# A transformer block pair on one core: norms and modulation go piece by piece into the operand's split, the feed-forward norm's reciprocal multiplies the first product's result, and first panels go tile by tile

## Chip, cores and metric

The kernel runs on one core of one Trainium2 chip. The metric is the device time of one execution in microseconds; the median of three runs is given. The profile is one execution of the same program.

## What is computed

One input of 256 tokens by 1024 features goes through two blocks. The first has an RMS norm, a state-space branch, an attention branch, gates and a feed-forward part. The second has two layers, each with a modulation of its input, three branches and a layer norm. What the change touches:

```
h = h + merged @ w_out                                   # first block
hid = relu(rmsnorm(h, norm_mlp) @ w_ff1)
h = h + (hid * hid) @ w_ff2
h = rmsnorm(h, norm_final)
for l in 0, 1:                                           # second block
    u = h * (1 + scale) + shift                          # shift, scale, gate: c_act @ w_ada + b_ada
    proj = u @ w_in                                      # q_lat, kv_lat, k_rope, ... are columns of proj
    ...
    h = layer_norm(ALPHA * h + gate * (m @ w_o), ln_g, ln_b)
```

`rmsnorm(x, g) = x * rsqrt(mean(x * x) + eps) * g`.

## The kernel before, in words

Activations stand transposed: features over the 128 partitions in 8 tiles (KT), 256 tokens in the free dimension. `h` is the residual stream. Every product is exact to about fp32 by three fp32r matmuls per tile (`three`, L1573 to L1575): both weights and operand are split in a high half (a rounding copy to fp32r) and a low half (value minus high half).

Weights come in panels, mostly 1024 rows by 256 columns (1 MB). The program `schedule` writes the order of everything by hand into one list; each engine walks through that list and executes its own part of each step. So the order of the list is the order in each engine's queue. A panel has five stages: SP loads it into one of four raw slots (L651); scalar makes the high half `w_hi` (L803); vector (L1082), or for `gate`, `ff1` and `ff2` GpSimd (L711), makes the low half `w_lo`; TensorE waits for that low half and does 48 matmuls of 256 columns in two column blocks (`blocks`); scalar or vector empties the bank. The halves of a panel are made ahead, by `next_splits`: at the step of a weight panel up to the panel three further in `w_hi`'s three slots and under four further in the index of all panels, at the step of an `ada` panel under two further in the index. The `ada` panels (the modulation's weights) count in the index, though they are not split; TensorE multiplies them as they land.

The operand is split too. `u_hi`, `u_lo` (L782, L1091) are shared by all panels of a stage and made in four pieces of two tiles. `low` makes one piece of the low half once scalar has its high half. The first panel of a stage waits for the four pieces at its tiles 0, 2, 4, 6 of the first column block.

Stages around the change:

- Start: `norm(0)`: scalar squares, TensorE sums with a matrix of ones (L1663), scalar takes the root (L782, with a table load), vector the reciprocal (L1127), then eight multiplies (L1140) into `tmp`, four high and four low pieces.
- Feed-forward (`ff1`, `ff2`): `out` panels add to `h` (L1109); `norm_steps(1, "u2", 14)` sets three `ada` panels between the last sum and the first `ff1` panel, while the norm goes on. Then eight chunks of two `ff1` and two `ff2` panels. Vector takes relu of a bank (L1356), scalar squares it and makes its high half, vector the low half.
- Into layer 0 of the second block: `norm_steps(2, ("u", 0), 17)`: the last norm of the first block writes into `h`, then `modulate(0)` on vector (L1418) makes `tmp`, whose rows vector subtracts the high half from, while scalar makes the same rows from `h` straight into `u_hi`.
- Into layer 1: `ln(0)` multiplies `h` by `rstd` (L1545); `modulate(1)` as above, with the layer norm's gain and bias folded into scale and shift by `modulate_columns(1)`.
- `prescale` (layer 0) or `ln_affine` (layer 1) multiply `h` by ALPHA on scalar, beside the latent sums.

The low half of the panel after `ada` panels (`ff1` 0, `q_lat` 0) is made in the step of the last of these three. In the list this is after `norm` or `ln`, and before `modulate`.

## Time and profile before

| | |
|---|---|
| median of three runs | 1257.37 us (1255.42 to 1257.55) |
| the profiled execution | 1257.67 us, span 1255.9 us |
| TensorE matmul busy | 1097.3 us, 87% |
| vector busy | 762.3 us, 61% |
| scalar busy | 536.6 us, 43% |
| GpSimd busy | 253.0 us, 20% |
| mean granted TensorE clock | 0.909 |

The span is the time from the first to the last instruction; the run's time has 1.8 us around it. TensorE is the busiest engine, but its busy time holds matmuls at two clock levels. Where it idles, the profile names what it waited for; where the granted clock is below 1, its matmuls start further apart.

### The profile page before, as it was taken

To read this page: it belongs to the slowest core of one execution; us is meant where nothing else is said; L and a number is where in the kernel's file an instruction comes from. 1 tells how busy PE (TensorE), PEld (TensorE's weight loads), DVE (VectorE), ACT (ScalarE), POOL (GpSimd) and SP (SyncE) were. 2 spreads that over 40 slices of the span, in tenths; PEclk is the share of its full clock that TensorE was granted. 3 is DMA by queue.
4 is the path that set the end of the run, shared out by engine and by line. 5 is a ranking of instruction groups with operands and counts; after the bars stand their busy time and mean duration, and the time that the engine had idled before them with its cause. 6 is when DMAs were issued, how large, how long until landed. Compare 5 with 4: busy or idle time off the path is not lost.

```text
span 1255.9 us, 19600 instructions
## 1 busy us (share of the span) xinstructions
PE 1097.3 (87%) x8120; PEld 1012.5 (81%) x8120; DVE 762.3 (61%) x1111; ACT 536.6 (43%) x613; POOL 253.0 (20%) x125
## 2 busy tenths in 40 slices
PE   5989779788989999979968798999799688989995
PEld 4976557667889999969867698998688687889985
DVE  4947556655353523255687788665556977795652
ACT  4533334253244444345423363643465132635432
POOL 2094753000078878700000000000000000000000
PEclk7977797788989999989979899999899788999998
DMA  7532332165566565545523345464447142545610
GB/s 250 186 102 90 112 125 77 68 201 180 167 195 197 168 200 169 182 128 190 172 68 101 101 143 161 136 213 153 131 139 235 38 131 76 160 137 166 202 35 33
DMA packets 159431, 179.53 MB, mean 143 GB/s; under 512 B 4976, under 2 KB 141680, under 8 KB 159344
## 3 DMA queue, kind: packets, MB, share of 16 engines
q1 hardware_dynamic: 159024, 177.22, 44.6%
q8 instruction: 64, 1.05, 0.4%
q0 software_dynamic: 320, 1.07, 0.2%
q14 instruction: 23, 0.19, 0.0%
HBM read 177.23 MB, written 1.05 MB: 142 GB/s over the span
## 4 chain that ended last, share of the span: by engine, by line
PE 58%; DVE 23%; issue 7%; ACT 7%; POOL 3%; DMA 1%; DVEq 0%; SPq 0%; ACTq 0%; POOLq 0%
PE pg L1573 17%; PE pg L1574 16%; PE pg L1575 16%; DVE area L1473 7%; DVE area L1091 5%; ACT w_hi L803 3%; DVE w_lo L1082 3%; ACT area L782 2%; DVE area L1099 2%; PE p_y L1729 1%; PE p_s L1663 1%; DVE mx L1494 1%; PE p_s L1712 1%; DVE area L1109 1%; DMA raw<-in_w_in 1%
## 5 line engine op out<-in xcount | busy, mean ns | idle before, releaser
L1573 PE MATMUL pg<-u_hi,w_hi 128*128 128x256 f32 x1664 | 497.7, 299 | 40.3 <-DVE u_lo L1091 36.0
L1574 PE MATMUL pg<-u_lo,w_hi 128*128 128x256 f32 x1664 | 487.3, 293 | 0.0
L1575 PE MATMUL pg<-u_hi,w_lo 128*128 128x256 f32 x1664 | 486.3, 292 | 0.0
L1573 PEld LDWEIGHTS pg<-u_hi,w_hi 128*128 128x128 f32 x1664 | 336.5, 202 | 53.0 <-issue 44.7
L1574 PEld LDWEIGHTS pg<-u_lo,w_hi 128*128 128x128 f32 x1664 | 336.8, 202 | 0.8
L1575 PEld LDWEIGHTS pg<-u_hi,w_lo 128*128 128x128 f32 x1664 | 335.9, 202 | 0.0
L1082 DVE TENSOR_TENSOR w_lo<-raw,w_hi 128x2048 fp32r<-128x2048 f32 (+3 forms) x109 | 241.2, 2218 | 115.0 <-ACT w_hi L803 114.8
L803 ACT ACTIVATE w_hi<-raw 128x2048 fp32r<-128x2048 f32 (+2 forms) x147 | 272.5, 1857 | 79.7 <-issue 38.6
L711 POOL TENSOR_TENSOR w_lo<-raw,w_hi 128x2048 fp32r<-128x2048 f32 x38 | 175.9, 4646 | 220.5 <-ACT w_hi L803 220.5
L809 ACT ACTIVATE area<-pg 128x512 f32<-128x512 f32 (+2 forms) x92 | 54.0, 587 | 168.9 <-PE pg L1575 156.9
L1473 DVE SCALAR_TENSOR_TENSOR area<-area,par 128x256 f32<-128x256 f32 x240 | 97.8, 479 | 0.8
L1573 PE MATMUL pg<-vb_hi,w_hi 128*128 128x256 f32 (+1 forms) x320 | 90.8, 284 | 1.4 <-POOL w_lo L711 0.9
L1575 PE MATMUL pg<-vb_hi,w_lo 128*128 128x256 f32 (+1 forms) x320 | 90.5, 283 | 0.0
L1574 PE MATMUL pg<-vb_lo,w_hi 128*128 128x256 f32 (+1 forms) x320 | 90.4, 282 | 0.0
L1573 PE MATMUL pg<-va_hi,w_hi 128*128 128x256 f32 x288 | 84.1, 292 | 1.8 <-DVE w_lo L1082 0.8
L1574 PE MATMUL pg<-va_lo,w_hi 128*128 128x256 f32 x288 | 83.3, 289 | 0.0
L1575 PE MATMUL pg<-va_hi,w_lo 128*128 128x256 f32 x288 | 83.1, 289 | 0.0
L1091 DVE TENSOR_TENSOR area<-area 128x512 f32<-128x512 f32 (+7 forms) x86 | 55.0, 639 | 30.7 <-ACT area L809 27.3
L782 ACT ACTIVATE area<-area 128x384 f32<-128x384 f32 (+6 forms) x67 | 37.1, 553 | 79.3 <-DVE area L1356 50.1
L1109 DVE TENSOR_TENSOR h<-pg,h 128x512 f32<-128x512 f32 x36 | 24.9, 691 | 66.5 <-PE pg L1575 65.6
L782 ACT ACTIVATE area<-area,nmax 128x128 f32<-128x128 f32 (+1 forms) x32 | 14.5, 455 | 112.7 <-DVE nmax L1095 112.2
L1573 PEld LDWEIGHTS pg<-vb_hi,w_hi 128*128 128x128 f32 (+1 forms) x320 | 60.0, 187 | 2.1 <-POOL w_lo L711 1.1
(211 smaller groups left out, 1338.3 us busy)
## 6 DMA issues: line engine op xcount, KB each, us to landing
raw<-in_w_in SPq DMA_DIRECT2D x68, 1024.0 KB, 5.5
raw<-in_w_ff SPq DMA_DIRECT2D x32, 1024.0 KB, 5.6
raw<-in_w_ada SPq DMA_DIRECT2D x24, 1024.0 KB, 5.2
raw<-in_w_gate SPq DMA_DIRECT2D x8, 1024.0 KB, 7.7
raw<-in_w_o SPq DMA_DIRECT2D x8, 1024.0 KB, 5.2
raw<-in_w_out SPq DMA_DIRECT2D x4, 1024.0 KB, 6.6
raw<-in_w_b_out SPq DMA_DIRECT2D x4, 1024.0 KB, 5.1
raw<-in_w_c_out SPq DMA_DIRECT2D x4, 1024.0 KB, 5.6
```

The costliest lines, as they stand in the source:

```text
L711: pool.tensor_tensor(w_lo[:, s, 0:n], raw[:, r, 0:n], w_hi[:, s, 0:n].bitcast(F32), ALU.subtract).then_inc(sem(f"raw_free{r}"), 1)
L782: return act.activation(out_, in_, func, **kw)
L803: act.activation(w_hi[:, q["s"] % HL, 0:n], raw[:, q["index"] % RAW, 0:n], ACT.Copy).then_inc(*c.event("w_hi", q["s"]))
L809: act.activation(dst, src, func, **kw).then_inc(*c.bank_free(g))
L1082: dve.tensor_tensor(w_lo[:, s, 0:n], raw[:, r, 0:n], w_hi[:, s, 0:n].bitcast(F32), ALU.subtract).then_inc(sem(f"raw_free{r}"), 1)
L1091: return dve.tensor_tensor(out_, a, b, op)
L1099: return dve.scalar_tensor_tensor(out=out_, in0=a, scalar=s, in1=b, op0=op0, op1=op1)
L1109: dve.tensor_tensor(out_, a, b, op).then_inc(*c.bank_free(g))
L1473: ins = dve.scalar_tensor_tensor(out=acc[:, j, :], in0=apad[:, j, k:k + T], scalar=w, in1=acc[:, j, :], op0=ALU.mult, op1=ALU.add)
L1573: pe.matmul(dst, w_h, x_h, start=first, stop=False)
L1574: pe.matmul(dst, w_h, x_l, start=False, stop=False)
L1575: return pe.matmul(dst, w_l, x_h, start=False, stop=last_)
```

## The change

1. `blocks`: where a panel waits for more than one piece, the order is by tile first and column block second, so that 12 matmuls instead of 6 can follow each piece. The start flag is set only by the very first.
2. The feed-forward norm. `u2_piece(j)`: scalar writes h times the gain into `u_hi`, vector the low half straight from h. No reciprocal is in it; it is multiplied to the relu of `ff1`'s result. The sums, root and reciprocal come after the pieces. The `ada` panels 15 and 16 move behind `ff1` 0 and 1.
3. `scaled`: vector multiplies `h` by `rstd` in four pieces, and makes the low halves between. The last norm of the first block no longer has its gain in `h`; it goes into the modulation's columns and into `prescale`, as in layer 1.
4. `modulate` moves from vector to scalar: two Identity into `tmp` and one Copy into `u_hi` a piece.

```diff
@@ def norm_steps
         ada_panel(i + 2)
         step("ada_turn", i + 1)
-        if k == 2:
-            step("modulate", 0)
-        step("split", key)
+        step("modulate", key[1])
         step("ada_take", i + 2)
@@ schedule, before and in the feed-forward
-    norm_steps(1, "u2", 14)
+    step("u2_piece", 0)
+    ada_panel(14)
+    norm_sums(1, 3)
+    for j in range(1, 4):
+        step("u2_piece", j)
+    step("ada_take", 14)
+    step("norm", 1)
     chunks = DFF // W
     for c in range(chunks + 1):
         if c < chunks:
             for n in range(2):
                 panel("ff1", 0, 2 * c + n, "w_ff1", 0, W * c + 256 * n, KT, 256, 1)
-                if (c, n) == (0, 0):
+                if c == 0:
+                    step("ada_turn", 14 + n)
+                    ada_panel(15 + n)
+                    step("ada_take", 15 + n)
+                if (c, n) == (1, 0):
                     step("ada_turn", 16)
                     step("ada_end", 1)
@@ scalar
+            def u2_piece(j, _):
+                if j == 0:
+                    act.wait_ge(sem("groups"), OPERANDS["u2"]["after"] + 1)
+                for s, v in emptied([groups_of("out")[j]]):
+                    act.wait_ge(s, v)
+                for i in (2 * j, 2 * j + 1):
+                    fn(u_hi[:, i, :], h[:, i, :], ACT.Identity, scale=col("norm_mlp", i)).then_inc(*(c.event("hi", "u2", j) if i % 2 else c.step()))
+
+            def modulate(l, _):
+                o = OPERANDS["u", l]
+                act.wait_ge(sem("groups"), o["after"] + 1)
+                act.wait_ge(sem("scale1"), over("scale1", l))
+                for j in range(4):
+                    act.wait_ge(sem("ln_rows"), over("ln_rows", l - 1, j))
+                    for i in (2 * j, 2 * j + 1):
+                        fn(tmp[:, i, :], h[:, i, :], ACT.Identity, bias=shift1[:, i:i + 1],
+                           scale=scale1[:, i:i + 1]).then_inc(*c.step())
+                    fn(u_hi[:, 2 * j:2 * j + 2, :], tmp[:, 2 * j:2 * j + 2, :], ACT.Copy).then_inc(*c.event("hi", ("u", l), j))
@@ scalar, prescale
-                act.wait_ge(sem("rows"), over("rows", ("u", l), 3))
-                fn(h[:, :, :], h[:, :, :], ACT.Copy, scale=ALPHA).then_inc(*c.event("alpha_h", l))
+                for j in range(KT):
+                    fn(h[:, j, :], h[:, j, :], ACT.Identity, scale=rest_g[:, j:j + 1]).then_inc(*(c.event("alpha_h", l) if j == KT - 1 else c.step()))
@@ vector: norm(k) calls scaled(-1) for k == 2, ln(l) calls scaled(l)
+            def scaled(l):
+                before = c.last
+                for j in range(4):
+                    dve.wait_ge(*before)
+                    dve.tensor_tensor(h[:, 2 * j:2 * j + 2, :], h[:, 2 * j:2 * j + 2, :], spread(rstd[:, 0, :], P, 2, T),
+                                      ALU.mult).then_inc(*c.event("ln_rows", l, j))
+                    if j and l < LAYERS - 1:
+                        low(("u", l + 1), j - 1)
+                if l < LAYERS - 1:
+                    low(("u", l + 1), 3)
+
+            def u2_piece(j, _):
+                dve.wait_ge(sem("hi"), over("hi", "u2", j))
+                for i in (2 * j, 2 * j + 1):
+                    stt(u_lo[:, i, :], h[:, i, :], col("norm_mlp", i), u_hi[:, i, :].bitcast(F32), ALU.mult,
+                        ALU.subtract).then_inc(*(c.event("lo", "u2", j) if i % 2 else c.step()))
@@ vector, panel, job ff1
-                    dve.tensor_scalar(tmp[:, f:f + 2, :], both, 0.0, None, ALU.max).then_inc(*c.bank_free(g))
+                    dve.scalar_tensor_tensor(out=tmp[:, f:f + 2, :], in0=both, scalar=0.0, in1=spread(rstd[:, 0, :], P, 2, T),
+                                             op0=ALU.max, op1=ALU.mult).then_inc(*c.bank_free(g))
@@ TensorE, blocks
-                for i, (a, m) in enumerate(widths):
-                    for k in range(q["kt"]):
-                        if i == 0 and k in waits:
-                            pe.wait_ge(*waits[k])
-                        ins = three(pg[g % 2][0:m, i * T:i * T + T], wh[:, k, a:a + m], wl[:, k, a:a + m],
-                                    x_hi[:, k, :], x_lo[:, k, :], k == 0, k == q["kt"] - 1)
+                turns = [(i, k) for i in range(len(widths)) for k in range(q["kt"])]
+                mixed = len(waits) > 1
+                if mixed:
+                    turns.sort(key=lambda at: at[1])
+                for i, k in turns:
+                    a, m = widths[i]
+                    if i == 0 and k in waits:
+                        pe.wait_ge(*waits[k])
+                    ins = three(pg[g % 2][0:m, i * T:i * T + T], wh[:, k, a:a + m], wl[:, k, a:a + m],
+                                x_hi[:, k, :], x_lo[:, k, :], k == 0 and not (mixed and i),
+                                (i, k) == turns[-1] if mixed else k == q["kt"] - 1)
```

`modulate_columns(0)` now also runs, in the third chunk of the feed-forward: it puts the last norm's gain into `scale1` and `rest_g`, and `shift1` is copied.

## Rows read from the trace of the kernel before

**Rows 1.** Busy engines (the page), and TensorE's waits (total, times, longest us).
```profile
PE 1097.3 (87%) x8120; PEld 1012.5 (81%) x8120; DVE 762.3 (61%) x1111; ACT 536.6 (43%) x613; POOL 253.0 (20%) x125
PE pg L1573 <- DVE u_lo L1091: 36.0, 6, 9.1
```
**Rows 2.** Timelines around F: start us, us, what, idle before, releaser.
```profile
337.20 0.69 DVE L1109 TENSOR_TENSOR h<-pg,h 128x512 f32<-128x512 f32 x1 [5.92 <-PE pg L1575]
337.93 0.63 ACT L782 ACTIVATE area<-h 128x512 f32<-128x512 f32 x1 [5.98 <-DVE h L1109]
339.62 1.28 ACT L782 ACT_TABLE_LOAD   x1
341.94 1.90 ACT L803 ACTIVATE w_hi<-raw 128x2048 fp32r<-128x2048 f32 x1
343.92 4.49 POOL L711 TENSOR_TENSOR w_lo<-raw,w_hi 128x2048 fp32r<-128x2048 f32 x1 [124.08 <-ACT w_hi L803]
350.03 0.55 PE L1573 MATMUL pg<-u_hi,w_hi 128*128 128x256 f32 x1 [6.87 <-DVE u_lo L1091]
359.96 0.39 PE L1573 MATMUL pg<-u_hi,w_hi 128*128 128x256 f32 x1 [0.59 <-POOL w_lo L711]
```
**Rows 3.** Clock by stretch: PE, PEld, DVE, ACT, POOL busy, clock, DMA share, GB/s.
```profile
350.10:356.10 6.00, 6.00 (x26) 5.60 (x27) 3.44 (x7) 4.32 (x5) 0.80 (x1) 0.50 0.53 192
556.50:561.00 4.50, 4.50 (x20) 4.39 (x21) 3.14 (x7) 4.01 (x8) 0.00 (x0) 0.50 0.46 160
```
**Rows 4.** Timeline of TensorE at M, the first `w_o` panel of layer 0.
```profile
860.53 0.35 PE L1573 MATMUL pg<-u_hi,w_hi 128*128 128x256 f32 x1 [3.08 <-DVE u_lo L1091]
...
861.20 0.28 PE L1575 MATMUL pg<-u_hi,w_lo 128*128 128x256 f32 x1
861.31 0.41 PE L1573 MATMUL pg<-u_hi,w_hi 128*128 128x256 f32 x1
861.52 0.41 PE L1574 MATMUL pg<-u_lo,w_hi 128*128 128x256 f32 x1
```
**Rows 5.** Vector: L1140 and L1109 (min/median/max ns), and the relu of 360 to 545.
```profile
L1140 DVE SCALAR_TENSOR_TENSOR area<-h,par,rows x16: 471/478/4775, 19.6 to 351.8; 128x256 f32<-128x256 f32 x16
L1109 DVE TENSOR_TENSOR h<-pg,h x31: 690/691/693, 381.0 to 537.8; 128x512 f32<-128x512 f32 x31
L1356 DVE TENSOR_SCALAR area<-pg 128x512 f32<-128x512 f32 x15 | 10.4, 691 | 45.1 <-PE pg L1575 44.9
```
**Rows 6.** Timelines around Q0, and the landing time of `w_in` loads (the page).
```profile
546.53 1.75 DVE L1127 RECIPROCAL rows<-root 128x256 f32<-128x256 f32 x1 [5.17 <-ACT root L782]
547.13 1.90 ACT L803 ACTIVATE w_hi<-raw 128x2048 fp32r<-128x2048 f32 x1
551.49 2.28 DVE L1082 TENSOR_TENSOR w_lo<-raw,w_hi 128x2048 fp32r<-128x2048 f32 x1
556.41 0.55 PE L1573 MATMUL pg<-u_hi,w_hi 128*128 128x256 f32 x1 [8.06 <-DVE u_lo L1091]
raw<-in_w_in SPq DMA_DIRECT2D x68, 1024.0 KB, 5.5
```
**Rows 7.** Timelines around Q1.
```profile
899.41 5.45 ACT L782 ACTIVATE u_hi<-h,shift,scale 128x256 fp32r<-128x256 f32 x8
900.44 2.28 DVE L1082 TENSOR_TENSOR w_lo<-raw,w_hi 128x2048 fp32r<-128x2048 f32 x1
904.96 0.55 PE L1573 MATMUL pg<-u_hi,w_hi 128*128 128x256 f32 x1 [5.81 <-DVE u_lo L1091]
```
**Rows 8.** Timelines: `prescale`, `ln_affine`, and TensorE behind the latter.
```profile
578.50 1.91 ACT L782 ACTIVATE h<-h 128x2048 f32<-128x2048 f32 x1
926.86 5.46 ACT L782 ACTIVATE h<-h,rest_b,rest_g 128x256 f32<-128x256 f32 x8
941.31 0.39 PE L1573 MATMUL pg<-u_hi,w_hi 128*128 128x256 f32 x1 [0.56 <-DVE w_lo L1082]
```
**Rows 9.** Timeline of TensorE's weight loads at S: a wait for the second piece.
```profile
23.73 0.29 PEld L1573 LDWEIGHTS pg<-u_hi,w_hi 128*128 128x128 f32 x1 [0.17 <-DVE u_lo L1091]
```

More of the change, by code:

```diff
@@ L236, in schedule @@
             step("rope_tables")
+            step("modulate_columns", 0)
     for j in range(3):
@@ L335, in schedule @@
             step("modulate", 1)
-            step("split", ("u", 1))
             step("ada_take", 23)
@@ L823, in split @@
                     act.wait_ge(sem("groups"), o["after"] + 1)
-                if isinstance(key, tuple) and key[0] == "u":
-                    l = key[1]
-                    act.wait_ge(sem("scale1"), over("scale1", l))
-                    for j in range(KT):
-                        if l == 0:
-                            act.wait_ge(sem("h_rows"), over("h_rows", j))
-                        else:
-                            act.wait_ge(sem("ln_rows"), over("ln_rows", l - 1, j // 2))
-                        fn(u_hi[:, j, :], h[:, j, :], ACT.Identity, bias=shift1[:, j:j + 1],
-                           scale=scale1[:, j:j + 1]).then_inc(*(c.event("hi", key, j // 2) if j % 2 else c.step()))
-                    return
                 if key == "ctx":
@@ L1046, in ln_affine @@
                     if l < LAYERS - 1:
-                        act.wait_ge(sem("rows"), over("rows", ("u", l + 1), j // 2))
                         fn(h[:, j, :], h[:, j, :], ACT.Identity, bias=rest_b[:, j:j + 1],
@@ L1054, in ln_affine @@
                            bias=col(("ln_b", l), j), scale=col(("ln_g", l), j)).then_inc(*c.event("affine", l, j))
-            steps = dict(split_ahead=split_ahead, silu=silu, norm_squares=norm_squares, norm=norm, ada_take=ada_take, ln_centre=ln_centre,
+            steps = dict(split_ahead=split_ahead, silu=silu, norm_squares=norm_squares, norm=norm, ada_take=ada_take, ln_centre=ln_centre, u2_piece=u2_piece, modulate=modulate,
                          ln_affine=ln_affine, split=split, panel=panel, gate_ahead=gate_ahead, s5_sines=s5_sines, s5_turn=s5_turn, s5_y=s5_y, s5_inner=s5_inner,
@@ L1130, in norm @@
                 invert(("norm", k))
-                name = ("norm_mix", "norm_mlp", "norm_final")[k]
                 if k == 0:
                     dve.wait_ge(sem("par_landed"), 16)
-                key = ("u0", "u2", None)[k]
+                    before = c.last
+                    for j in range(KT):
+                        dve.wait_ge(*before)
+                        ins = dve.scalar_tensor_tensor(out=tmp[:, j, :], in0=h[:, j, :], scalar=col("norm_mix", j), in1=rstd[:, 0, :],
+                                                       op0=ALU.mult, op1=ALU.mult)
+                        ins.then_inc(*(c.event("rows", "u0", j // 2) if j % 2 else c.step()))
+                        if j % 2 and j >= 3:
+                            low("u0", j // 2 - 1)
+                    low("u0", 3)
+                elif k == 2:
+                    scaled(-1)
+            def scaled(l):
                 before = c.last
-                for j in range(KT):
+                for j in range(4):
                     dve.wait_ge(*before)
-                    dst = tmp[:, j, :] if k < 2 else h[:, j, :]
-                    ins = dve.scalar_tensor_tensor(out=dst, in0=h[:, j, :], scalar=col(name, j), in1=rstd[:, 0, :],
-                                                   op0=ALU.mult, op1=ALU.mult)
-                    ins.then_inc(*(c.event("h_rows", j) if k == 2 else c.event("rows", key, j // 2) if j % 2 else c.step()))
-                    if k < 2 and j % 2 and j >= 3:
-                        low(key, j // 2 - 1)
-                if k < 2:
-                    low(key, 3)
+                    dve.tensor_tensor(h[:, 2 * j:2 * j + 2, :], h[:, 2 * j:2 * j + 2, :], spread(rstd[:, 0, :], P, 2, T),
[9 more added lines that the diff above has]
+                        ALU.subtract).then_inc(*(c.event("lo", "u2", j) if i % 2 else c.step()))
             S = lambda k: small[:, k, :]
@@ L1541, in ln @@
                 invert(("var", l))
-                before = c.last
-                for j in range(4):
-                    dve.wait_ge(*before)
-                    dve.tensor_tensor(h[:, 2 * j:2 * j + 2, :], h[:, 2 * j:2 * j + 2, :], spread(rstd[:, 0, :], P, 2, T),
-                                      ALU.mult).then_inc(*c.event("ln_rows", l, j))
+                scaled(l)
             dve.wait_ge(sem("const"), over("const", "all"))
```

28 lines of the change are left out of this document (10 added, 18 removed).

## Prediction

> **What bounds the kernel now.** I first read the engine shares: TensorE is busy 1097.3 us of 1255.9, vector 762.3 [rows 1]. TensorE sets the pace, so an edit is worth what it does to TensorE's idle time and clock. Then the waits of TensorE: its largest entry is 36.0 us in six waits of a weight panel for `u_lo`, the low half of the shared operand [rows 1]. The change touches exactly the six places of these waits. I call them by what follows: S (first panel), F (feed-forward), Q0 and Q1 (first panel of layers 0 and 1 of the second block), M (`w_o`, twice). TensorE idles 6.87 us before F, 8.06 before Q0, 5.81 before Q1, 3.08 before M [rows 2, 4, 6, 7]. Third, the granted clock after them: it is 0.50 from 350.1 to 356.1 and from 556.5 to 561.0 [rows 3], the level of 1.2 GHz; after Q1's idle time it lasts to about 909. Neighbouring matmuls start 0.21 us apart at the low level, 0.12 at the high one [rows 4]. A panel of 48 takes 5.8 us at the high level, and each microsecond spent at the low level costs 0.44 us (4.7 matmuls, worth 0.56). Last, the timelines of vector, scalar and GpSimd at the five kinds of place give the order of things.
>
> **F before.** Sum, table load, root, reciprocal, rows. TensorE starts `ff1` 0 at 350.03 and ends it near 358.9; `ff1` 1 starts at 359.96, when GpSimd has its low half [rows 2], so `ff1` 2 ends two panels later, near 371.6.
>
> **F after.** `u2_piece` needs no norm. The last `out` group ends near 337.1, its rows are in h at 337.89 [rows 2]. Scalar: an Identity of one tile takes 0.68 in a row of eight (5.46) [rows 8], so piece 0 stands at 338.45, the square (0.63) [rows 2] at 339.1, pieces 1 to 3 at 340.5, 341.9, 343.2. Vector adds two steps of 0.48 [rows 5] and a handover: low halves at 339.5, 341.5, 342.9, 344.3. The weights of `ff1` 0 are early: it is now three places behind `out` 2 instead of six, so its high half is made in that step and GpSimd is through near 331. TensorE ends the sums at 340.2 and takes 12 matmuls (1.44) a piece, at the high level: 341.7, 343.15, 344.6, 346.05. That is 12.8 us earlier than 358.9, by the norm's chain taken off the path and the new order of tiles.
>
> Most of it is lost again at once. `ff1` 1 is four places behind `out` 3 and the look-ahead takes less than four. So its high half is made in the step of `ff1` 0, and scalar comes to that after the pieces (343.2), `ada_take` 14 (0.4), the table load (1.28) [rows 2] and the root (0.4): 345.4. High half 1.90, to 347.3; GpSimd 4.49, a little more in steady state, to 352.0 [rows 2]. TensorE has `ada` 15 behind it at 347.4: a new idle time of 4.6 us. I expect the clock to fall: the idle times of 5.81 to 8.06 did that, and even 3.08 before M was followed by starts 0.21 apart [rows 4]. Taking 4.7 us at the low level, as after Q0, costs 2.1. So `ff1` 1 ends at 359.9, `ada_turn` and `ada` 16 at 361.3, `ff1` 2 at 367.0, one more turn makes 367.4 against 371.6. **Gain 4.2 us.** Bounds: 6.3 if the clock stays high, 3 if it is low for 6.1 us as after F before, and GpSimd late by half a microsecond.
>
> The relu now multiplies by `rstd` too. No row shows this form. Below: the relu itself, 0.691, and the addition of a bank and an SBUF tile, 0.691 as well. Above: two half-width scalar_tensor_tensor, 0.96 [rows 5]. I take 0.7, the nearest row being the addition with its two operands of the same kinds. It is hidden: vector idled 45.1 us before 15 relus [rows 5]; without that cover the upper bound would make 16 x 0.27 = 4.3 us. GpSimd, busy in most of this stretch, might hold it: a multiply on two SBUF operands at F lasted 4.775 (median 0.478). But the 31 additions from 381 to 538, with a bank and an SBUF tile, never took over 0.693 [rows 5]. I take no hold.
> The Trainium skill (SBUF — State Buffer, "SBUF: two separate sides") states a lock between vector and GpSimd, and for a vector instruction not in a fast mode names two SBUF inputs as its condition. By that rule the new multiply, with one input in PSUM, runs free and the sum stays; a rule without this condition would speak against the change and give case (c) below. The trace agrees with the page: 4.775 for two SBUF inputs, 0.693 at most for one.
>
> **Q0 and Q1.** Before, vector did the norm's rows, then `w_lo` of the first panel (2.28, at 551.49 and 900.44), then modulation and low halves [rows 6, 7]. Now `scaled` does the rows and all four `low` calls, inside `norm` or `ln`. The first panel's `w_lo` belongs to the step of an `ada` panel further down, so in vector's queue it stands behind all four pieces. And pieces are slower: scalar makes them alone, two Identity and a Copy (0.68 + 0.68 + 0.72 with its gap), 2.1 us each, 8.4 for four. Before, scalar's share was 5.45 [rows 7].
> Q0: scalar is free at 549.05, the first rows stand at 549.0 (reciprocal to 548.3, one step of 0.7) [rows 6]. Pieces end at 551.2, 553.3, 555.4, 557.4; last low half 558.15; `w_lo` to 560.4. TensorE starts at 560.5 instead of 556.41, 4.1 later, and no longer waits between pieces (about 0.4 before). **Loss 3.7 us.** Bounds 2.8 and 5: the time at the low level may be 1 us shorter or 2 longer, and the pieces a little off.
> Q1: scalar starts at 899.41 as before [rows 7]. Last piece 907.8, low half 908.5, `w_lo` 910.75, TensorE at 910.85 instead of 904.96: 5.9, less 0.2 of waits inside. **Loss 5.7 us**, bounds 4.5 and 6.9.
> Behind the waiting `low` calls vector has only this `w_lo` and later ones queued, and TensorE alone waits for them. Scalar's queue has `ada_take` and the next high halves behind the pieces; they are done (about 561 in Q0) well before TensorE, now at 568, wants them. On SP's queue the load into the raw slot that is freed 7 to 10 us later belongs to the fourth panel after, over 15 us on; it lands in 5.5 [rows 6]. Free. The tile order gives nothing here, since every piece is there at the start.
>
> **The rest.** `prescale` is 8 steps, 5.46, instead of one of 1.91. Layer 1 does that already, and there TensorE idles 0.56 at 941.31; layer 0 has no such gap [rows 8]. Loss 0.6, bounds 0 and 1.2. `modulate_columns(0)`, five small steps, lies in F, where vector idles: nothing. S: each wait for a piece costs 0.1 to 0.2 at the low level [rows 9], some 0.5 in three; the new order takes them away. Gain 0.3, bounds 0 and 0.6. M: no piece is waited for after the first, TensorE being slower (six matmuls 1.28) than the pieces come (0.8): nothing, bounds 0 and 0.2. `out` 0 has all pieces in advance. The last `scaled(1)` is the old code.
>
> **Sum**, against this execution (1257.67: span 1255.9 and 1.8 around it; the median of three is 1257.37, 0.3 less): -0.3 - 4.2 + 3.7 + 5.7 + 0.6 = +5.5, so **1263.2**. All good ends together give +0.2 (-0.8 - 6.3 + 2.8 + 4.5 + 0, 1257.9), all bad ones +10.1 (1267.8).
>
> **The rivals.**
> (a) Faster. The first panel's `w_lo` isn't behind the pieces but between or before them, and TensorE takes 12 matmuls as each piece comes. Then Q0 starts at 552.0 and ends at 560.3, not 564.4 (-4.1), and Q1 ends at 910.0, not 912.8 (-2.8); sum -0.3 - 4.2 - 4.1 - 2.8 + 0.6 = -10.8, 1246.9. For it: before, `w_lo` came right behind the rows [rows 6, 7], and scalar's half was made by 549.03. Against it: the `low` calls now stand ahead of it in one queue. The point from which it decides is the start of `w_lo` before the last `u_lo`. Chance 0.10.
> (b) No change. The stall before `ff1` 1 doesn't come, because its high half is made before table load and root; F gains 4.6 + 2.1 more, 1256.5. Against it: in the old trace too the high half came after the table load (339.62, 341.94) [rows 2]. Chance 0.12.
> (c) Still slower. The relu's multiply is held by GpSimd as the norm's was. A hold is 4.3 at most; with half of it hidden by the other bank for a quarter of the sixteen, 8 to 9 more, 1272. Against it: the additions [rows 5]. Chance 0.06.
> The forecast keeps 0.72.
>
> **From this to the numbers.** The likeliest case gives 1263.2. The range of 8 in 10 goes from 1256.5, which takes in (b) and my lower bound, to 1268.5, above my upper bound; (a) and (c) stay out. A measurement of this kernel tells about 0.2% (2.5 us) from no change: faster is under 1254.9, slower over 1259.9. Faster: (a) and a little of (b), 0.12. Same: the rest of (b) and my low end, 0.16. Slower: 0.72.
>
> **What the new profile would show.** F: `ff1` 0 starts near 340 with no idle time of note, then one of 4 to 5 us released by GpSimd's `w_lo`. Q0 and Q1: TensorE idles about 12 us and is released by vector's `w_lo`, no longer by `u_lo`. The relu's rows stay near 0.7. If TensorE's wait at Q0 still ends with `u_lo`, or `ff1` 1 follows without a gap, the prediction is wrong.

## The result and the profile after

The changed kernel takes 1262.67 us (median of 20 runs, 1255.54 to 1270.18). The kernel before takes 1257.48 in the 20 runs beside it. The ratio is 1.0043, with a 95% interval of 1.0025 to 1.0061: slower by 5.2 us, where 5.5 was forecast. The profiled execution of the changed kernel took 1261.53; its span is 1259.8, against 1255.9.

First the engine shares of the changed kernel and, from the view of TensorE's waits, the entries of weight panels (total us, times, longest).

```profile
PE 1098.5 (87%) x8120; PEld 1012.3 (80%) x8120; DVE 746.9 (59%) x1089; ACT 545.8 (43%) x632; POOL 252.9 (20%) x125
```
```profile
PE pg L1594 <- DVE w_lo L1097: 24.0, 5, 11.7
PE pg L1594 <- DVE u_lo L1106: 15.8, 3, 9.7
```

Before, one entry of 36.0 us named `u_lo` [rows 1]. Now 24.0 us name vector's `w_lo`, the low half of a weight panel, and `u_lo` keeps 15.8 in three waits. TensorE's busy time grew by 1.2 us (0.1%), the span by 3.9: most of the difference is idle time, and it has a new releaser.

F. Timelines of the changed kernel for scalar, vector, GpSimd and TensorE (start us, us, what, idle before and its releaser), in this order.

```profile
335.04 1.05 ACT L790 ACTIVATE u_hi<-h,par 128x256 fp32r<-128x256 f32 x2 [5.25 <-PE pg L1596]
336.18 0.63 ACT L790 ACTIVATE area<-h 128x512 f32<-128x512 f32 x1
336.91 3.34 ACT L790 ACTIVATE u_hi<-h,par 128x256 fp32r<-128x256 f32 x6
340.36 0.39 ACT L817 ACTIVATE root<-pg 128x256 f32<-128x256 f32 x1
340.84 1.28 ACT L790 ACT_TABLE_LOAD   x1
342.14 0.38 ACT L790 ACTIVATE root<-p_s 128x256 f32<-128x256 f32 x1
342.42 1.90 ACT L811 ACTIVATE w_hi<-raw 128x2048 fp32r<-128x2048 f32 x1
```
```profile
335.04 0.69 DVE L1124 TENSOR_TENSOR h<-pg,h 128x512 f32<-128x512 f32 x1 [5.92 <-PE pg L1596]
344.42 0.69 DVE L1389 SCALAR_TENSOR_TENSOR area<-pg,rows 128x512 f32<-128x512 f32 x1
```
```profile
344.40 9.52 POOL L719 TENSOR_TENSOR w_lo<-raw,w_hi 128x2048 fp32r<-128x2048 f32 x2 [15.91 <-ACT w_hi L811]
```
```profile
348.97 0.38 PE L1594 MATMUL pg<-u_hi,w_hi 128*128 128x256 f32 x1 [3.89 <-POOL w_lo L719]
```

The idle 6.87 us ahead of `ff1` 0 [rows 2] are gone: `ff1` 0 runs from 337.65 to 343.74 without a pause. Behind it and the short `ada` 15 TensorE stands still from 345.08 on for 3.89 us. The rows say why, read backwards: it waits for GpSimd's low half, which began at 344.40; that waited for the high half of 342.42 on scalar, and ahead of it in scalar's queue stand the pieces, `ada_take` 14 (scalar empties that panel's bank), the table load and the root, one right after the other from 336.91 on.

The two first panels of the second block, TensorE's timeline:

```profile
552.53 0.58 PE L1594 MATMUL pg<-u_hi,w_hi 128*128 128x256 f32 x1 [11.73 <-DVE w_lo L1097]
...
907.97 0.58 PE L1594 MATMUL pg<-u_hi,w_hi 128*128 128x256 f32 x1 [11.10 <-DVE w_lo L1097]
```

and vector's timeline ahead of Q0:

```profile
540.76 1.29 DVE L1167 TENSOR_TENSOR h<-h,rows 128x512 f32<-128x512 f32 x2
543.62 0.69 DVE L1106 TENSOR_TENSOR u_lo<-area,u_hi 128x512 fp32r<-128x512 f32 x1 [1.57 <-ACT u_hi L790]
...
549.58 0.69 DVE L1106 TENSOR_TENSOR u_lo<-area,u_hi 128x512 fp32r<-128x512 f32 x1 [1.29 <-ACT u_hi L790]
550.19 5.62 DVE L1097 TENSOR_TENSOR w_lo<-raw,w_hi 128x2048 fp32r<-128x2048 f32 x3
```

The idle time was 8.06 and 5.81 us and ended with `u_lo` [rows 6, 7]. Now it is 11.73 and 11.10 and ends with `w_lo`. Vector was through with the rows' first half at 542.05 and then waited for scalar before each of four low halves, 4.2 us in all, with `w_lo` behind them in its queue though its input had been ready since 541.57. This is what the forecast named.

Where the 3.9 us of span come from, by landmarks that both traces have (the last sum of `out` into `h`, the start of TensorE's idle time at Q0 and at Q1, and the first matmul of the sums of the latents, the norm that follows `q_lat`):

| landmark | before | after | difference so far | the stretch itself |
|---|---|---|---|---|
| last sum of `out` | 337.20 | 335.04 | -2.2 | -2.2 |
| idle time at Q0 begins | 548.35 | 540.80 | -7.6 | F: -5.4 |
| sums of the latents, layer 0 | 578.46 | 574.85 | -3.6 | Q0: +3.9 |
| idle time at Q1 begins | 899.15 | 896.87 | -2.3 | +1.3 |
| sums of the latents, layer 1 | 926.82 | 930.08 | +3.3 | Q1: +5.5 |
| end of span | 1255.9 | 1259.8 | +3.9 | +0.6 |

The first line isn't the change's. The experiment `block2_part_only`, whose code up to there is the old one, has the same landmark at 334.99, and `tiles_only`, which has the new start, has it at 337.20. The granted clocks from 12 to 30 us differ (0.54 before, 0.72 in the changed kernel, 0.72 and 0.54 in these two). The +1.3 between the latents and Q1 isn't a term of the change either. It holds a stretch of low clock, 575.1 to 578.5, which the kernel before doesn't have there: the ten matmuls of the sums take 4.11 us instead of 2.43. Six of the fourteen traces have such a stretch at these sums, `ff_part_only` among them, whose `prescale` is the old one, so it doesn't come with the eight steps. Rows of the changed kernel by stretch (busy us of PE, PEld, DVE, ACT and POOL, then granted clock, DMA share, GB/s):

```profile
350.00:353.50 3.50, 3.50 (x19) 3.50 (x19) 0.00 (x0) 1.91 (x1) 3.50 (x1) 0.54 0.94 306
353.50:357.00 3.50, 3.50 (x36) 3.40 (x39) 0.49 (x1) 0.00 (x0) 3.50 (x2) 1.00 0.01 4
552.50:558.30 5.80, 5.77 (x28) 5.78 (x29) 3.31 (x2) 0.29 (x1) 0.00 (x0) 0.52 0.80 245
575.30:578.70 3.40, 3.40 (x11) 2.69 (x9) 0.00 (x0) 3.17 (x8) 0.00 (x0) 0.53 0.63 173
908.00:913.20 5.20, 5.20 (x25) 5.20 (x26) 3.25 (x2) 0.23 (x1) 0.00 (x0) 0.52 0.82 248
```

After the new idle time at F TensorE restarted at 348.97; the clock was at its low level (1.2 GHz) from 349.8 for about 3.4 us, and then at the high one (2.4 GHz): 19 matmuls in 3.5 us, then 36.

### The profile page after: what moved, and what is told of

Its sections match the earlier page's. It is cut to its first block, busy times and chain, and to the rows that moved or that the text cites. A ratio compares the mean times of both kernels' runs of the same rounds, so it can differ in the third digit from the quotient of the medians.

```text
span 1259.8 us, 19580 instructions
## 1 busy us (share of the span) xinstructions
PE 1098.5 (87%) x8120; PEld 1012.3 (80%) x8120; DVE 746.9 (59%) x1089; ACT 545.8 (43%) x632; POOL 252.9 (20%) x125
## 4 chain that ended last, share of the span: by engine, by line
PE 58%; DVE 23%; ACT 8%; issue 7%; POOL 3%; DMA 1%; DVEq 0%; SPq 0%; ACTq 0%; POOLq 0%
PE pg L1594 16%; PE pg L1595 16%; PE pg L1596 16%; DVE area L1498 7%; DVE area L1106 5%; ACT w_hi L811 4%; DVE w_lo L1097 3%; ACT area L790 2%; DVE area L1114 2%; PE p_s L1690 2%; PE p_y L1756 1%; PE p_s L1588 1%; DVE mx L1519 1%; PE p_s L1739 1%; DVE area L1124 1%
## 5 line engine op out<-in xcount | busy, mean ns | idle before, releaser
L1106 DVE TENSOR_TENSOR area<-area 128x512 f32<-128x512 f32 (+7 forms) x86 | 55.0, 639 | 30.2 <-ACT area L817 26.5
```

Source lines behind the costliest of these rows:

```text
L1106: return dve.tensor_tensor(out_, a, b, op)
```

## The experiments

### The two halves of the change, each alone

`ff_part_only` is the kernel before with everything at F: `u2_piece`, the new order of steps, the relu that multiplies by `rstd`, and the tile order of first panels. `block2_part_only` has only the second block's part: the modulation of both layers on scalar, the columns of layer 0 made earlier, `scaled` with its `low` calls, and the eight steps of `prescale`.

```diff
 ff_part_only, against before
-    norm_steps(1, "u2", 14)
+    step("u2_piece", 0)
+    ada_panel(14)
+    norm_sums(1, 3)
+    for j in range(1, 4):
+        step("u2_piece", j)
+    step("ada_take", 14)
+    step("norm", 1)
...
 block2_part_only, against before
+        if k == 2:
+            step("modulate", 0)
+        else:
+            step("split", key)
...
-                fn(h[:, :, :], h[:, :, :], ACT.Copy, scale=ALPHA)
+                for j in range(KT):
+                    fn(h[:, j, :], h[:, j, :], ACT.Identity, scale=rest_g[:, j:j + 1])
```

> The kernel before with the feed-forward part of the change (pieces of the operand without the norm, reciprocal in the relu, ada panels 15 and 16 moved) and the tile order, nothing of the second block. My theory: TensorE idles about 4 us before ff1 1 instead of 6.9 before ff1 0, the place gives 4.2 to 5.5 us, the tile order about 1 more (waits between pieces at the start and before both q_lat panels gone): 1251 to 1252.5. Rival, that the multiply on rstd is held by GpSimd: relu rows of over 1 us and no gain, 1257 or more.

> The changed kernel with the feed-forward part and the tile order put back: only scaled, the modulation on scalar, the columns and prescale in eight steps. My theory: TensorE idles about 12 us before each first q_lat panel (8.1 and 5.8 before), released by vector's w_lo; 3.7 + 5.7 + 0.6 to 1.7, so 1267 to 1269. Rival, that the loss of the whole change comes from somewhere else (clock phases, the feed-forward part): 1257 to 1260.

Measured: `ff_part_only` 1254.04 (1251.59 to 1255.78, ratio 0.9965, interval 0.9953 to 0.9978), `block2_part_only` 1273.89 (1268.03 to 1274.44, ratio 1.0108, interval 1.0089 to 1.0126). TensorE's timeline in both:

```profile
348.10 0.39 PE L1603 MATMUL pg<-u_hi,w_hi 128*128 128x256 f32 x1 [3.88 <-POOL w_lo L721]
547.99 0.55 PE L1603 MATMUL pg<-u_hi,w_hi 128*128 128x256 f32 x1 [8.07 <-DVE u_lo L1110]
```
```profile
557.77 0.58 PE L1596 MATMUL pg<-u_hi,w_hi 128*128 128x256 f32 x1 [11.66 <-DVE w_lo L1090]
914.17 0.58 PE L1596 MATMUL pg<-u_hi,w_hi 128*128 128x256 f32 x1 [11.09 <-DVE w_lo L1090]
```

So the change has two parts of opposite sign, and each stall belongs to one: the one before `ff1` 1 to F's part, the 11.66 and 11.09 us to the second block's.

The gain of F's part is 4.0 us between the medians, where 5.5 to 7 were expected. In its trace the stretch from the last sum of `out` to Q0 takes 205.7 us against 211.2, the same 5.4 less as in the changed kernel. Most of the rest is lost between the latents of layer 0 and Q1, in steps that this edit doesn't touch: TensorE does the same 2188 matmuls there in 4.4 us more, at a lower mean clock (0.93 against 0.95). First the kernel before, then `ff_part_only`:

```profile
578.46:899.15 320.69, 288.48 (x2188) 270.86 (x2188) 227.66 (x333) 137.02 (x158) 0.00 (x0) 0.95 0.43 136
```
```profile
570.44:895.53 325.09, 293.68 (x2188) 274.72 (x2188) 227.69 (x333) 137.03 (x158) 0.00 (x0) 0.93 0.43 134
```

Over the fourteen traces this stretch takes from 320.7 to 326.2 us.

The loss of the other part is 13.6 by the ratio (15.8 between the medians), where the forecast's terms make 10.0. Its six runs stand in two groups, 1268.0 (twice) and 1273.7 to 1274.4 (four times). The mean granted clock is 0.905 in the first group and 0.897 to 0.900 in three of the four others; the profiled execution belongs to the first, so no row says where the second group's time arises. In this trace Q0 costs 3.1 us and Q1 5.8, which confirms the forecast's terms of 3.7 and 5.7. Another 3.1 lie between the latents and Q1, in the stretch of the rows above.

### The cause at Q0 and Q1: the order in vector's queue

The theory: the first panel's `w_lo` is late because the four waiting `low` calls stand ahead of it. The rival: the pieces are late anyway, since scalar now makes them alone. `wlo_first` puts `w_lo` ahead of the four `low` calls in the changed kernel, behind all four multiplies, and leaves the pieces to scalar. `wlo_behind` puts the new order into the kernel before and leaves its faster pieces.

```diff
 wlo_first, against the changed kernel, in scaled
-                    if j and l < LAYERS - 1:
-                        low(("u", l + 1), j - 1)
...
-                    low(("u", l + 1), 3)
+                    low_halves(first_splits(ahead[0] + 1, ahead))
+                    for j in range(4):
+                        low(("u", l + 1), j)
...
 wlo_behind, against before: in vector's split_ahead, and at the end of its modulate
+                if (job, l, n) in (("ada", 1, 7), ("ada", 1, 11)):
+                    return
...
+                low_halves(first_splits(ahead[0] + 1, ahead))
```

> The changed kernel; in scaled all four multiplies come first, then w_lo of the first q_lat panel, then the four low calls. My theory, that the wait behind the pieces is the cause: TensorE starts the panel about 7 us earlier, right after the first piece, takes 12 matmuls a piece and ends some 8 us earlier at both places; the idle time before it is about 5 us; 1246 to 1249. Rival, that scalar's slower pieces (2.1 us each) are the cause and not the order on vector: TensorE has to wait for the last piece anyway, 1260 to 1263.

> The kernel before with one edit: vector makes w_lo of the first q_lat panel of both layers behind its modulation and the four low halves, as the change does, with the faster pieces of before. My theory, that the order is the larger share: TensorE starts 3.9 and 3.6 us later and saves 0.3 in waits: 1258 plus 7, 1264 to 1266. Rival, that scalar's slower pieces are the larger share: under 3 us, 1259 to 1261.

Measured: `wlo_first` 1250.26 (1248.17 to 1254.33; ratio 0.9938, interval 0.9924 to 0.9953), `wlo_behind` 1266.26 (1259.14 to 1267.55; ratio 1.0055, interval 1.0035 to 1.0075). Timelines of `wlo_first`, TensorE and then vector:

```profile
546.01 0.55 PE L1594 MATMUL pg<-u_hi,w_hi 128*128 128x256 f32 x1 [5.41 <-DVE u_lo L1106]
...
897.01 0.55 PE L1594 MATMUL pg<-u_hi,w_hi 128*128 128x256 f32 x1 [4.32 <-DVE u_lo L1106]
```
```profile
540.57 2.50 DVE L1167 TENSOR_TENSOR h<-h,rows 128x512 f32<-128x512 f32 x4
542.98 2.28 DVE L1097 TENSOR_TENSOR w_lo<-raw,w_hi 128x2048 fp32r<-128x2048 f32 x1
545.18 1.48 DVE L1106 TENSOR_TENSOR u_lo<-area,u_hi 128x512 fp32r<-128x512 f32 x2
```

and TensorE's timeline of `wlo_behind`:

```profile
560.48 0.58 PE L1576 MATMUL pg<-u_hi,w_hi 128*128 128x256 f32 x1 [12.14 <-DVE w_lo L1082]
```

The other order is worth 12.4 us in the changed kernel (6.6 at each of the two places by the landmarks): the wait goes from 11.73 to 5.41 at Q0 and from 11.10 to 4.32 at Q1, and `u_lo` releases again. The last low half is hardly earlier than in the changed kernel (549.39 against 549.58), so the pieces didn't become faster; TensorE now works on piece 0 while scalar makes the others. In the other direction the order costs 7 us by the ratio (8.7 between the medians) with the faster pieces of the kernel before. By the landmarks it costs 3.4 at Q0 and 3.7 at Q1, of the 3.9 and 5.5 of the whole change. So the order is the larger share, and the slower pieces are the smaller one.

Where both are as before at Q0 the stretch from the start of the idle time to the latents' sums takes 30.1 us, with both new 34.0, and with the new pieces and `w_lo` first 27.5: less than before. This isn't the tile order's work: from the restart to the sums TensorE needs 22.0 us before and 22.1 in `wlo_first`, and the 2.6 us lie in the idle time ahead of it (8.06 and 5.41). Vector's rows of the kernel before show them:

```profile
548.32 3.25 DVE L1140 SCALAR_TENSOR_TENSOR h<-h,par,rows 128x256 f32<-128x256 f32 x8
...
553.89 0.17 DVE L1095 TENSOR_SCALAR scale<-ada 128x8 f32<-128x8 f32 x1
554.09 1.38 DVE L1418 TENSOR_SCALAR area<-h,scale,shift 128x256 f32<-128x256 f32 x4
555.58 0.69 DVE L1091 TENSOR_TENSOR u_lo<-area,u_hi 128x512 fp32r<-128x512 f32 x1
```

From the end of the reciprocal to the first low half vector needed 7.3 us; in `wlo_first` it needs 4.6, because the columns are made earlier, the modulation is scalar's, and the rows take 2.50 us instead of 3.25. So the move of work off vector does shorten the path to the first piece, once `w_lo` isn't stuck behind it. Whether the tile order is needed to hide scalar's slower pieces was not tried; no run takes it away from this kernel.

### The stall before `ff1` 1

`ada_later` moves the panels `ada` 15 and 16, which lay behind `ff1` 0 and `ff1` 1, one place down each, so that fewer panels stand between GpSimd's work and its use.

```diff
-                if c == 0:
-                    step("ada_turn", 14 + n)
-                    ada_panel(15 + n)
-                    step("ada_take", 15 + n)
-                if (c, n) == (1, 0):
+                if (c, n) in ((0, 1), (1, 0)):
+                    step("ada_turn", 14 + c)
+                    ada_panel(15 + c)
+                    step("ada_take", 15 + c)
+                if (c, n) == (1, 1):
```

> The changed kernel; ada 15 comes behind ff1 1 and ada 16 behind ff1 2, so that ff1 1 is within the look-ahead at out 3 and its low half is done before the norm's chain on scalar. My theory: the 3.9 us of idle time before ff1 1 and its 3.4 us of low clock go, perhaps 1 us comes back before ff1 3: 4 to 5.4 us under the changed kernel, 1257 to 1259. Rival, that the idle time only moves to ff1 2 (GpSimd as the bound): no change, 1261 to 1263.

Measured: 1257.51 (1254.69 to 1260.23, ratio 0.9999, interval 0.9988 to 1.001), 5.2 under the changed kernel. TensorE has no idle time between `ff1` 0 and 1; the longest in this stretch is 0.94, before `ff1` 3:

```profile
361.63 0.38 PE L1594 MATMUL pg<-u_hi,w_hi 128*128 128x256 f32 x1 [0.94 <-POOL w_lo L719]
```

The forecast priced the stall at 4.6 and the clock behind it at 2.1. Row by row the stall is 3.89, and 3.4 us at the low level come to 1.5, by the price of a low microsecond in the forecast: 5.4, near the 5.2 between the medians. By the landmarks less is won: from the last sum of `out` to Q0 this kernel takes 201.9 us and the changed one 205.8, 3.9 less, and two smaller waits that come back (0.47 before `ff1` 2, and the 0.94 above) make up nearly all of the difference.

### The relu's multiply, the eight steps of `prescale`, the tile order

Three terms of the sum that were taken as small or nothing, each alone. `relu_plain` is the changed kernel with the plain relu, so the feed-forward's result lacks the factor `rstd`; the other two are the kernel before with one edit.

```diff
 relu_plain, against the changed kernel
-                    dve.scalar_tensor_tensor(out=tmp[:, f:f + 2, :], in0=both, scalar=0.0, in1=spread(rstd[:, 0, :], P, 2, T),
-                                             op0=ALU.max, op1=ALU.mult)
+                    dve.tensor_scalar(tmp[:, f:f + 2, :], both, 0.0, None, ALU.max)
...
 prescale_eight, against before
-                fn(h[:, :, :], h[:, :, :], ACT.Copy, scale=ALPHA)
+                for j in range(KT):
+                    fn(h[:, j, :], h[:, j, :], ACT.Copy, scale=ALPHA)
...
 tiles_only, against before, in TensorE's panel
+                mixed = len(waits) > 1
+                if mixed:
+                    turns.sort(key=lambda at: at[1])
```

> The changed kernel with the old relu in ff1; the multiplication by rstd is left out of the computation. My theory: the rows of the relu are 0.69 us in both and there is no difference, 1261 to 1264. Rival, that the multiply costs something in the wait of bank or GpSimd: 1258 or less.

> The kernel before with prescale as eight steps with the constant factor. My prediction's 0.6 us, by the gap of layer 1: 1258.2, hardly to be told from 1257.5; what tells is whether TensorE has a gap of about 0.56 near 593. Rival, since no such gap stands in the trace of the changed kernel: 0.

> The kernel before with the tile order in blocks alone. My theory: only the waits between pieces go, 0.3 at the start, 0.3 to 0.4 each at the feed-forward and before both q_lat panels: 1 to 1.5 us, 1256. Rival, that it lets the panel end with the last piece plus 12 matmuls and so gives 2 us or more a place: 1250 or less.

Measured: `relu_plain` 1262.79 (1261.93 to 1268.46), 0.1 from the changed kernel; `prescale_eight` 1257.2 against 1258.24 (ratio 0.999, interval 0.998 to 1.0001); `tiles_only` 1256.26 (ratio 0.9981, interval 0.9966 to 0.9996). The relu's rows by shape, of the changed kernel and of `relu_plain` (busy us, mean ns, idle before):

```profile
L1389 DVE SCALAR_TENSOR_TENSOR area<-pg,rows 128x512 f32<-128x512 f32 x16 | 11.1, 692 | 55.0 <-PE pg L1596 54.7
```
```profile
L1389 DVE TENSOR_SCALAR area<-pg 128x512 f32<-128x512 f32 x16 | 11.1, 692 | 55.0 <-PE pg L1595 54.7
```

The multiply costs nothing, on vector itself and in the end: same duration, same idle time around it, and from the last sum of `out` to the end both traces take 924.8 us. GpSimd never held it (the rival (c)), though it was at a low half of a weight panel in all sixteen cases. The eight steps cost nothing either: TensorE has no idle time behind `prescale` in layer 0. What makes the gap of 0.56 at 941.31 in layer 1 [rows 8] was not tried; the changed kernel, with the same eight `ln_affine` steps, has none from 930.08 to 960. What the tile order gives by itself is at the edge of what can be measured: the ratio says 2.4 us, but the trace of `tiles_only` has every landmark within 0.2 us of the kernel before. Where TensorE waits for `w_lo` behind the last piece it can give nothing.

### Both stalls mended, and one step further

`both_mended` has both edits, of `wlo_first` and `ada_later`. `halves_early` goes on from it: scalar makes the first `q_lat` panel's high half ahead of the norm's table load and root, and vector makes the low half before the norm's reciprocal, where it idles 5.17 us for the root; at Q1 it makes it between the second and third of the four multiplies.

```diff
 halves_early, against both_mended: in the list of steps
+        step("next_halves", 0)
...
 on scalar
+            def next_halves(place, _):
+                high_halves(first_splits(ahead[0] + 1, ahead))
...
 on vector
+            def next_halves(place, _):
+                if place == 0:
+                    low_halves(first_splits(ahead[0] + 1, ahead))
```

> wlo_first and ada_later together. If the two mended places are independent the sum of both: 1250.3 less 4 to 5.4, so 1245 to 1246.5. If the feed-forward gain is lost later (in the wait for weights or at the norm): 1249 to 1251.

> both_mended, and both halves of the first q_lat panel come earlier still: at layer 0 the high half on scalar before ada 17's take and the low half on vector before the reciprocal, where both engines idle; at layer 1 the high half straight after the root and the low half between the second and third multiply by rstd. My theory: TensorE's start is now set by the first piece alone, 2 us earlier at layer 0 and 1 at layer 1: 1244 to 1245. Rival, that the low clock level after the restart takes up what the earlier start gives: 1246.5 to 1247.5.

Measured: `both_mended` 1247.09 (1245.59 to 1248.13; ratio 0.9912, interval 0.9898 to 0.9926), `halves_early` 1239.73 (1237.33 to 1244.95; ratio 0.9853, interval 0.9831 to 0.9874). TensorE at Q0 in `halves_early`, and vector's rows ahead of it:

```profile
535.61 0.36 PE L1604 MATMUL pg<-u_hi,w_hi 128*128 128x256 f32 x1 [3.59 <-DVE u_lo L1115]
```
```profile
530.19 1.75 DVE L1151 RECIPROCAL rows<-root 128x256 f32<-128x256 f32 x1 [0.38 <-ACT root L792]
531.98 2.50 DVE L1176 TENSOR_TENSOR h<-h,rows 128x512 f32<-128x512 f32 x4
534.77 0.69 DVE L1115 TENSOR_TENSOR u_lo<-area,u_hi 128x512 fp32r<-128x512 f32 x1 [0.29 <-ACT u_hi L792]
```

The idle time of vector ahead of its reciprocal is 0.38 instead of 5.17 [rows 6], the wait at Q0 3.59 instead of 5.41. Both kernels beat the two given ones. But `both_mended` gained only 3.2 on `wlo_first`, under what was expected; its landmarks say 3.5 from the last sum of `out` to Q0, so the sum of the two edits holds with the 3.9 of above and not with the 4 to 5.4 that were put in. And `halves_early` gained 7.4 on `both_mended`, more than expected, and this number is not the edit's alone. In `halves_early` the last sum of `out` stands at 330.14, in `both_mended` at 336.61, with no difference in code ahead of it. From there to the end the one takes 907.6 us, the other 908.4. From the start of the idle time to the latents' sums the stretch at Q0 takes 25.2 against 27.9, and the one at Q1 24.6 against 26.5. So the edit wins 2.7 and 1.9 us where it acts, and the stretch between the two places takes 4.2 more (326.2 against 322.0), 47 us of it at the low clock against 38.

### Who makes the pieces, and how far a median carries

`pieces_shared` is `halves_early` with the pieces made as in the kernel before: scalar writes `u_hi` itself, vector makes the sum again and subtracts.

```diff
-                        fn(tmp[:, i, :], h[:, i, :], ACT.Identity, bias=shift1[:, i:i + 1],
-                           scale=scale1[:, i:i + 1]).then_inc(*c.step())
-                    fn(u_hi[:, 2 * j:2 * j + 2, :], tmp[:, 2 * j:2 * j + 2, :], ACT.Copy)
+                        fn(u_hi[:, i, :], h[:, i, :], ACT.Identity, bias=shift1[:, i:i + 1],
+                           scale=scale1[:, i:i + 1])
...
+                        for i in (2 * j, 2 * j + 1):
+                            ts(tmp[:, i, :], h[:, i, :], scale1[:, i:i + 1], shift1[:, i:i + 1], ALU.mult, ALU.add)
```

> halves_early with the pieces made as before the change: scalar writes u_hi straight from h (two Identity a piece), vector makes the same rows again and subtracts. My theory, that the order and not the speed of the pieces costs: once w_lo is out of the way TensorE at the low level needs 2.56 us a piece, more than scalar's 2.1, so only the first piece counts: within 1.5 us of halves_early. Rival, that the slower pieces hold TensorE: 3 us or more faster than halves_early.

Measured: 1249.41 (1246.07 to 1250.18; ratio 0.9919, interval 0.9906 to 0.9933), 9.7 above `halves_early`. By that number the expectation missed. Where the edit acts it did not: the stretch at Q0 takes 25.4 against 25.2, that at Q1 25.3 against 24.6. From the last sum of `out` to the end both take 907.5 to 907.6, in which differences of 4.3 and 2.9 us in stretches that the edit doesn't touch nearly cancel. The 6.5 us between the two profiled executions (spans 1244.2 and 1237.7) stand ahead of 337, in code that is the same. So one kernel was timed again, unchanged, on another occasion.

> The same kernel as halves_early, word for word, on another occasion. In its first trace the last result row of the projection ahead of F came at 330.14 us, in the traces of both_mended and pieces_shared at 336.6, though no instruction ahead of F differs between the three; from that row to the end of the span the three took 907.6, 908.4 and 907.6. Theory 1, the early row belongs to the kernel (its layout of instructions or data shifts the arrival of the first loads and the stretches of low clock that follow): the row comes at 329 to 331 again, the median is 1237 to 1242. Theory 2, the early row was drawn with that occasion (its chip, its placement in memory): the row comes at 334 to 337, the median is 1243 to 1248, close to the two others, and then the edit of halves_early is worth about 1 us, not 7.

Measured: 1243.57 (1239.96 to 1248.03; ratio 0.9885, interval 0.9867 to 0.9903), and vector's timeline has the landmark here (first `halves_early`, then the repetition):

```profile
330.14 0.69 DVE L1133 TENSOR_TENSOR h<-pg,h 128x512 f32<-128x512 f32 x1 [5.92 <-PE pg L1606]
```
```profile
336.59 0.69 DVE L1133 TENSOR_TENSOR h<-pg,h 128x512 f32<-128x512 f32 x1 [5.92 <-PE pg L1606]
```

The early landmark is not the kernel's: the same kernel has it 6.5 us later. Whether it goes with the occasion, as the second theory says, or is drawn anew in each execution stays open. Only one execution was profiled each time, the runs spread over 7.6 and 8.1 us, and `prescale_eight` and `pieces_shared`, timed on the same occasion and chip as the first `halves_early`, have the landmark at 335.61 and 336.63. Vector's rows show where the 6.5 us arise. Here are two of its steps in the first execution, then in the second:

```profile
99.50 0.69 DVE L1115 TENSOR_TENSOR area<-p_bu,waves 128x512 f32<-128x512 f32 x1
113.11 0.69 DVE L1115 TENSOR_TENSOR area<-p_bu,waves 128x512 f32<-128x512 f32 x1 [1.03 <-PE p_y L1766]
```
```profile
100.59 0.69 DVE L1115 TENSOR_TENSOR area<-p_bu,waves 128x512 f32<-128x512 f32 x1
119.91 0.69 DVE L1115 TENSOR_TENSOR area<-p_bu,waves 128x512 f32<-128x512 f32 x1 [3.72 <-PE p_y L1766]
```

and the stretch from 99.6 to 113.2 us of both, the first execution first (the eighth number is the clock):

```profile
99.60:113.20 13.60, 13.60 (x92) 10.78 (x92) 11.71 (x20) 6.93 (x9) 8.85 (x5) 1.00 0.49 155
```
```profile
99.60:113.20 13.60, 12.69 (x42) 10.14 (x43) 9.88 (x16) 5.33 (x7) 9.75 (x6) 0.50 0.46 152
```

About 1.1 us comes from the first load, whose tiles arrive a little earlier (the last square of the start begins at 9.29 and at 10.62), and at 99.5 us the second execution is still just this 1.1 behind. At 113 it is 6.8 behind: in between its clock was at the low level for 13.6 us, where that of the first was at the high one, 42 matmuls against 92. Why the low stretches lie otherwise in the two executions no run shows. The best version is `halves_early` all the same: its two timings are 1.5% and 1.15% under the kernel before, and the two intervals together reach from 0.983 to 0.990. What it gains on `both_mended` lies between 0.1 and 0.8 us (the two traces, from the last sum of `out` to the end) and 3.5 to 7.4 (the medians), and more can't be said.

## Why the prediction was right

The total is 5.2 where 5.5 was said. The mechanisms are the ones given, and the releasers, the idle times and the order of the steps came as described. The closeness of the total is partly luck. In the traces the three large terms add to +4.1 (-5.4, +3.9 and +5.5), where they were put at +5.2, and `prescale` (0.6) and S (-0.3) gave nothing; what brings the median to 5.2 is time that none of the terms explains.

- Q0 +3.7: measured +3.9. The new releaser is the one named and the idle time is 11.73 where about 12 was said. `wlo_first` shows that the mechanism is the one given, the order of vector's queue.
- Q1 +5.7: measured +5.5. Idle 11.10, the same releaser.
- F -4.2: measured -5.4 by the landmarks, in the changed kernel and in `ff_part_only` alike (-4.0 between the latter's medians). The chain was right (scalar's queue of pieces, `ada_take`, table load, root, high half, then GpSimd), and every link of it is in the rows above. Two sizes were off. The clock behind the stall stayed low for 3.4 us, not 4.7; that the shorter idle time is the reason is not shown. And the pieces went faster: an Identity was priced at 0.68, gap included, from a row that has a bias and a scale, while `u2_piece` has a scale alone: six took 3.34, 0.56 each.
- The relu's multiply at nothing: right, 692 ns with it and without it.
- `prescale` +0.6: wrong, nothing. The forecast carried a gap over from layer 1 by its place, without having shown that the eight steps there make it.
- S -0.3 and M 0: M has its 3.08 as before. S shows nothing by the landmark (337.20 with and without the new order); the ratio of `tiles_only` is 2.4 us under before (0.5 to 4.3), which no landmark of its trace shows.
- Rival (a), 1246.9, is what `wlo_first` does (1250.26), and it had been priced 3 us too well. It put Q0 at -4.1 and Q1 at -2.8 against the kernel before; by the landmarks they are -2.6 and -1.0. It had TensorE start 3.65 us after the idle time begins at Q0. `wlo_first` starts after 5.41; only `halves_early`, where `w_lo` is made ahead of the reciprocal, comes to 3.59. Rival (b), 1256.5, fell with the stall of 3.89; `ada_later`, which takes that stall away, measures 1257.51. Rival (c) fell with the relu's 692 ns.

The agreement of 5.2 and 5.5 is closer than the measurement allows one to claim: the same code ahead of F differed by 6.5 us between two executions of one kernel, and by 2.2 between the two profiles that were compared.

## What to carry to other kernels

When steps are moved between engines, write down each in-order queue and ask what stands behind the first instruction that waits; here one 2.3 us instruction behind four waiting ones, at two places, cost 12.4 us together, and moving it ahead of them turned a loss into a gain of 0.6%. An operand that becomes ready earlier only moves the bound to the other operand of the same matmul: look for the one that is late next before you count the gain. And compare two kernels from landmark to landmark, first of all over the code that they share, since there the difference should be nothing and shows how much a median can tell. A stretch that an edit doesn't touch can also take a few microseconds more with the very same matmuls, so read the gain where the edit acts and look at the granted clock of the rest.

## What the runs showed of the hardware

- Restart after idle time. Before, TensorE ran at the low level for 6.2 us after its restart at F (idle 6.87) and for 4.6 at Q0 (idle 8.06); in the changed kernel for 5.5 at Q0 (idle 11.73) and 5.1 at Q1 (idle 11.10). The length of the idle time alone did not set it: after 11.66 to 11.73 us idle at Q0 the low level lasted 3.6 (`block2_part_only`), 5.5 and 6.0 us (`ada_later`), and after 8.06 to 8.07 us 3.8 (`prescale_eight`), 4.6 and 5.9 (`ff_part_only`). After 3.88 or 3.89 us idle at F it lasted 3.4 us in four traces of four, from 0.9 us behind the restart on; but after 4.32 at Q1 in `wlo_first` it lasted 5.6.
- The low stretches move between executions of the same code. The same kernel, profiled twice, differed by 6.5 us at 337 us, 5.7 of them built up between 99.5 and 113 us, where the clock was 0.50 in one and 1.00 in the other; the medians of the two timings differ by 3.8. The six runs of `block2_part_only` fell into two groups 6 us apart. What decides it is open.
- In these rows scalar's price for a 128x256 tile goes by the operands that are read per partition: 417 ns with neither (the Copy of `prescale_eight`), 509 with a scale (`u2_piece`), 600 with bias and scale (the pieces at Q0 and Q1). The rows (count, then busy us and mean ns of one) are of `prescale_eight` first, then of the changed kernel:

```profile
L782 ACT ACTIVATE h<-h 128x256 f32<-128x256 f32 x8 | 3.3, 417 | 0.3
```
```profile
L790 ACT ACTIVATE u_hi<-h,par 128x256 fp32r<-128x256 f32 x8 | 4.1, 509 | 5.7 <-PE pg L1596 5.2
L790 ACT ACTIVATE area<-h,shift,scale 128x256 f32<-128x256 f32 x16 | 9.6, 600 | 1.1
```

  The Trainium skill (ScalarE: Activation LUTs, "What ACT_TABLE_LOAD costs") gives about 93 ns for each such operand, and the rows agree: 92 and 91. An estimate with this figure would have put a tile of the pieces at F at 0.59 us (0.68 less 0.09), where 0.56 was measured.
- A vector instruction with one input in PSUM and one in SBUF wasn't held by GpSimd, which was busy during it: 692 ns in sixteen of sixteen. The Trainium skill (SBUF — State Buffer, "SBUF: two separate sides") names two SBUF inputs as the condition of the lock, and the row agrees.
